# The in-projection begun at half of the tokens, and the combine of the experts' rows shared between GpSimd and VectorE

## The chip, the cores and the metric

The kernel runs on one core of one Trainium2 chip. The metric is device time in microseconds (us) from launch to end; a lower number is better. Each run is one execution of the whole program. The profile is one execution recorded by the hardware profiler; its span goes from the first to the last instruction. The engines are TensorE (PE; its weight loads are PEld), VectorE (DVE), ScalarE (ACT), GpSimd (POOL) and SyncE (SP, which here only issues DMAs).

## What is computed

One inference step of a 2-layer decoder over 576 tokens (512 of a prompt, 64 samples), model width 1024, float32. Cut to what matters here:

```python
def decoder(x, ...):
    for l in range(2):
        mix = token_mixers(rmsnorm(x, norm1_g), ...)   # z = hn @ w_in, then RG-LRU | MLA | GLA, then @ w_out
        x = x + mix
        x = x + hier_moe(rmsnorm(x, norm2_g))
    return rmsnorm(x, final_norm_g), ...

def hier_moe(t):                                       # every token goes to 2 of 32 experts
    w_sel = softmax(top_v) * g_prob                    # two weights per token
    y = sum over the 2 choices k of  w_sel[:, k] * expert_k(t)
```

`hn` is the normalised input of the mixers, `z` (1792 columns here, with padding) the in-projection.

## The kernel before, in words

The program is written by hand per engine: each engine has its own instruction list, and semaphores order them. Nothing is scheduled by a planner, except that PSUM banks are dealt out by a list: `psum_plan` names every use of a bank in order, use n lies in bank n modulo 8, `begin` waits until the bank's former use was read, `done` says it is filled, `take` waits for that, `give` says it was read, and `after` waits for the reading.

Tokens lie in five tiles `t` of 128 rows (the last has 64) in `x`. A layer begins with `norm_sums` on ScalarE (L717 squares a tile and sums it, L718 takes the root) and `norm_rows` on VectorE (L974 the reciprocal, L975 the scaled row into `xs`). TensorE transposes each tile in two groups of four (L1498, keys `("hn", t, g)`), and the groups are copied from PSUM to `hT`: group 0 by ScalarE (L706, `half_out`), group 1 by VectorE (L998), the latter after all five tiles were normalised. Only then does the in-projection start.

The in-projection runs over 14 column tiles `m` in the order of `Z_ORDER`, and for each over two halves `h` of 288 tokens, eight matmuls a block (L1528, keys `("z", m, h)`; the trace has two records for each matmul). Weights come by DMA into four buffers in turn (`win`, L445); SP loads the fifth column tile when the first one's second half has been computed. ScalarE and VectorE read the blocks out of PSUM in the same order. VectorE has a chain of small coefficient instructions ahead of that (L1004 to L1019), which waits once for ScalarE (L768).

After the mixers and the router comes the loop over blocks of experts. It leaves every token's two expert rows in `y_rows` in HBM. When all are stored, SP loads them into `ygat` with ten DMAs (L534; n = 2t + k for tile t and choice k). VectorE then combines: for each tile two instructions `x = ygat * weight + x` (L1474), one per choice, the second waiting for the first, and a memset that tells the tile is done (`combined`). One tile late it normalises (`norm_rows`) for the next layer, or, after the second layer, for the output, which SP stores tile by tile (L540). GpSimd's last instruction of a layer is `hold` (L647).

On GpSimd other work of the same kind stands in the mixers: products of masks (L610), differences (L593, L627, L632), and a cast at the start (L551).

Of the kernel before, what the change touches and what calls it, by code (L numbers as in the profile page):

```python
# [61 lines left out]
def rows_of(t):  # L62
    return P if t < TT - 1 else NS
# [114 lines left out]
def hybrid_step(nc, a, o):  # L178
# [5 lines left out]
    with ExitStack() as ctx:  # L184
# [35 lines left out]
        def cut(region, at, *dims):  # L220
# [89 lines left out]
            qpe_ready gelu gexp oacc_ready oacc_steps gsq out_b sel_exp sel_exp_done held home_copied""".split()  # L310
# [238 lines left out]
        def _(pool):  # L549
# [3 lines left out]
            for L in range(DEPTH):  # L553
# [142 lines left out]
                hold()  # L696


        @block.scalar
        def _(act):  # L700
# [3 lines left out]
            def half_out(L, kind, t):  # L704
                bk, r = take(act, L, (kind, t, 0)), rows_of(t)
                give(copy(hT[:, 0:4, t * P:t * P + r],  # L706
                          bk[:, :].rearrange("p (k n) -> p k n", k=4)[:, :, 0:r]), (kind, t, 0))

            def norm_sums(n):

                junk = cut(rb, 0, D) if n % 2 == 1 else cut(rg, 0, D)
                for t in range(TT):
                    r = rows_of(t)
                    if n == 0:
                        act.wait_ge(x_in[t], 16)
                    x_done(act, n, t)
                    link(fn(junk[:r, :], x[:r, t, :], ACT.Square, accum_out=sm[:r, t:t + 1]))  # L717
                    fn(sm[:r, 5 + t:6 + t], sm[:r, t:t + 1], ACT.Sqrt, scale=1.0 / D, bias=eps_col[:r]) \  # L718
                        .then_inc(S["ssq_ready"], 1)
                    if n % 2 == 0 and n < 2 * DEPTH and t >= 2:  # L720
                        half_out(n // 2, "hn", t - 2)
# [40 lines left out]
            for L in range(DEPTH):  # L762
                norm_sums(2 * L)
                for t in range(TT - 2, TT):
                    half_out(L, "hn", t)
# [4 lines left out]
                for m in Z_ORDER:  # L770
                    for h, cols in enumerate(halves):
                        if m in (Z_CQ, Z_CQ + 1, Z_CKV):
                            bk = take(act, L, ("z", m, h))
                            fn(sq[:, m - Z_CQ, cols], bk[:, 0:HALF], ACT.Square).then_inc(S["sq_ready"], 1)
                        elif m < Z_Y:
                            bk, key = take(act, L, ("z", m, h)), ("z", m, h)
                            if h == 0:
                                give(copy(xext[:, m, 3:3 + HALF], bk[:, 0:HALF]), key)
                            else:
                                copy(xext[:, m, 3 + HALF:XE], bk[:, 0:SEQ - HALF])  # L780
                                give(copy(xext[:, m, XE:].rearrange("p (b c) -> p b c", c=SEXT)[:, :, 3:],
                                          bk[:, SEQ - HALF:HALF].rearrange("p (b q) -> p b q", q=NQ)), key)
                        elif m < Z_CQ:
                            bk = take(act, L, ("z", m, h))
                            give(copy(yl[:, m - Z_Y, cols], bk[:, 0:HALF]), ("z", m, h))
                        elif m in (Z_GV, Z_GV + 1):
                            bk = take(act, L, ("z", m, h))
                            give(copy(gv[:, m - Z_GV, cols], bk[:, 0:HALF]), ("z", m, h))
# [174 lines left out]
        def _(dve):  # L963
# [29 lines left out]
            for L in range(DEPTH):  # L993
                if L == 0:
                    norm_rows(0, range(TT))
                for t in range(TT):
                    bk, r = take(dve, L, ("hn", t, 1)), rows_of(t)
                    give(V.tensor_copy(hT[:, 4:8, t * P:t * P + r],  # L998
                                       bk[:, :].rearrange("p (k n) -> p k n", k=4)[:, :, 0:r]), ("hn", t, 1))
# [96 lines left out]
                for m in Z_ORDER:  # L1096
                    for h, cols in enumerate(halves):
                        key = ("z", m, h)
                        if m in (Z_CQ, Z_CQ + 1, Z_CKV):
                            bk = take(dve, L, key)  # L1100
                            nsq += 1
                            dve.wait_ge(S["sq_ready"], 6 * L + nsq)
                            give(V.tensor_copy(cq[:, m - Z_CQ, cols] if m < Z_CKV else ckvT[:, cols],
                                               bk[:, 0:HALF]), key)
                        elif m == Z_PE:
                            bk = take(dve, L, key)
                            if h > 0:
                                dve.wait_ge(S["kpe_ready"], 2 * L + h)
                            V.tensor_copy(gaT[64:80, cols], bk[64:80, 0:HALF])
                            link(V.tensor_copy(ropetmp[0:32, :], bk[32:64, 0:HALF]))  # L1110
                            link(V.tensor_tensor(ropetmp[0:32, :], ropetmp[0:32, :], sin[0:32, cols], ALU.mult))
                            give(V.tensor_tensor(kpeT[0:32, cols], bk[0:32, 0:HALF], cos[0:32, cols], ALU.mult),
                                 key)
                            after(dve, L, key)
                            V.tensor_tensor(kpeT[0:32, cols], kpeT[0:32, cols], ropetmp[0:32, :], ALU.add) \
                                .then_inc(S["kpe_ready"], 1)
                        elif m in (Z_GQ, Z_GK):
                            bk = take(dve, L, key)
                            give(V.tensor_copy((gq if m == Z_GQ else gk)[:, cols], bk[:, 0:HALF]), key)
                        elif m >= Z_GO:  # L1120
                            bk = take(dve, L, key)
                            dve.wait_ge(S["tailsaved"], L + 1)
                            give(V.tensor_copy(gout[:, m - Z_GO, cols], bk[:, 0:HALF]), key)
# [344 lines left out]
                for n in range(2 * TT):  # L1468
                    t, k = n // 2, n % 2
                    r = rows_of(t)  # L1470
                    dve.wait_ge(ygat_in[n], 16 * (L + 1))
                    if k == 1:
                        dve.wait_ge(S["ygat_used"], 2 * TT * L + n)
                    ins = V.scalar_tensor_tensor(x[:r, t, :], ygat[:r, n, :], sm[:r, 100 + 5 * k + t:101 + 5 * k + t],  # L1474
                                                 x[:r, t, :], ALU.mult, ALU.add)
                    ins.then_inc(S["ygat_used"], 1)
                    if k == 1:
                        dve.wait_ge(S["ygat_used"], 2 * TT * L + n + 1)
                        V.memset(sm[:, 205:206], 0.0).then_inc(S["combined"], 1)
                        if t > 0:  # L1480
                            norm_rows(2 * L + 2, (t - 1,))
# [4 lines left out]
        def _(pe):  # L1486
# [15 lines left out]
            for L in range(DEPTH):  # L1502
                transpose_rows(L, "hn", 2 * L, range(TT))
                for t in range(TT):
                    for g in range(2):
                        after(pe, L, ("hn", t, g))
# [15 lines left out]
                for n, m in enumerate(Z_ORDER):  # L1522
                    pe.wait_ge(win_in[n % 4], 16 * (L * WUSES[n % 4] + n // 4 + 1))
                    mrows = 80 if m == Z_PE else P
                    for h, cols in enumerate(halves):
                        bk = begin(pe, L, ("z", m, h))
                        for k in range(KT):
                            ins = mm(bk[:mrows, 0:HALF], win[:, n % 4, k, :mrows], hT[:, k, cols],  # L1528
                                     start=k == 0, stop=k == KT - 1)
                        done(ins, ("z", m, h))  # L1530
# [431 lines left out]
```

## Time and profile before

| what | us |
|---|---|
| median of 3 runs | 1673.18 |
| lowest and highest run | 1669.05, 1679.38 |
| profiled execution, its own time | 1666.96 |
| its span | 1665.0 |
| TensorE busy in the span | 1343.6 (81%) |
| VectorE busy | 584.1 (35%) |
| ScalarE busy | 368.3 (22%) |
| GpSimd busy | 306.1 (18%) |

Busy shares are averages over stages that have different limits; what a change in a stage is worth is read from the waits in that stage. The in-projection of layer 0 begins at 25.46 us and that of layer 1 at 834.17 us of the span. The last instructions of the span are the normalisation after layer 1 and the stores of the output.

### The profile page before, as it was taken

Reading aid. Unit: us, or ns where it says so; the run is one execution under the profiler, and the core shown is the slowest. Engines: PE = TensorE matmul, PEld = TensorE weight load, DVE = VectorE, ACT = ScalarE, POOL = GpSimd, SP = SyncE. Lnnn points to the kernel's source line nnn. Section 1 sums busy time; section 2 is a strip of 40 time slices with the busy share of each in tenths; the row PEclk is TensorE's granted clock in tenths of the full one; section 3 lists DMA queues with packets and bytes.
Section 4 is the critical chain, followed back from the end, with each engine's and each line's share of the span. In section 5 each row is a group of like instructions: output and inputs, shape, how many; then the busy total and the mean of one; then the engine's idle time right before and its main releaser. Section 6 shows DMA issues by size and latency. Waiting matters only on the chain.

```text
span 1665.0 us, 21687 instructions
## 1 busy us (share of the span) xinstructions
PE 1343.6 (81%) x7043; PEld 782.2 (47%) x7044; DVE 584.1 (35%) x1561; ACT 368.3 (22%) x849; POOL 306.1 (18%) x713
## 2 busy tenths in 40 slices
PE   5989999868975778888499899887799578788881
PEld 4767555434453344444277664544334434344440
DVE  3272587321134111111525537851022511111115
ACT  3242124423110011111214312352302011111112
POOL 0001410000001333333100034100000033343341
PEclk9999989879966999999699899998699589999996
DMA  6210120432074899996521012024123779989745
GB/s 227 64 34 26 59 76 1 152 127 89 20 309 162 332 392 369 407 407 236 199 79 60 23 53 84 1 76 145 71 76 112 301 272 406 389 308 356 298 194 176
DMA packets 98612, 298.51 MB, mean 179 GB/s; under 512 B 13198, under 2 KB 29934, under 8 KB 98162
## 3 DMA queue, kind: packets, MB, share of 16 engines
q1 hardware_dynamic: 85138, 272.62, 43.8%
q0 software_dynamic: 13408, 25.04, 4.1%
q8 instruction: 38, 0.62, 0.2%
q14 instruction: 28, 0.23, 0.0%
HBM read 289.37 MB, written 27.09 MB: 190 GB/s over the span
## 4 chain that ended last, share of the span: by engine, by line
PE 55%; DMA 20%; DVE 12%; issue 5%; ACT 3%; POOL 2%; SPq 1%; POOLq 1%; DVEq 0%; ACTq 0%
DMA ra<-h_rows,slot_now 18%; PE bank L1528 13%; PE bank L1788 9%; PE bank L1846 5%; PE bank L1857 3%; PE bank L1828 2%; PE bank L1733 2%; PE bank L1722 2%; PE bank L1721 2%; PE bank L1550 2%; PE bank L1801 2%; PE bank L1615 1%; PE bank L1665 1%; PE bank L1669 1%; DVE x L1474 1%
## 5 line engine op out<-in xcount | busy, mean ns | idle before, releaser
L1528 PE MATMUL bank<-ra,rb 128*128 128x288 f32 (+1 forms) x896 | 224.9, 414 | 3.6 <-DVE ra L998 3.6
L1528 PEld LDWEIGHTS bank<-ra,rb 128*128 128x128 f32 (+1 forms) x896 | 171.2, 192 | 54.6 <-issue 4.2
L1467 DVE COPY rb<-bank 128x512 f32<-128x512 f32 x71 | 49.1, 692 | 222.4 <-DMA y_rows<-rb,home_now 171.7
L957 ACT ACTIVATE rb<-bank 128x128 f32<-128x128 f32 x71 | 19.7, 277 | 415.6 <-PE bank L1846 415.6
L1828 PE MATMUL bank<-cst,ra 128*128 128x128 f32 x292 | 48.8, 291 | 72.9 <-DMA ra<-h_rows,slot_now 72.9
L1846 PE MATMUL bank<-rg,rb 128*64 128x256 f32 x768 | 92.2, 395 | 7.5 <-issue 4.5
L1461 DVE TENSOR_TENSOR rb<-rb,bank 128x128 f32<-128x128 f32 x71 | 20.5, 288 | 195.5 <-ACT rb L957 195.5
L1846 PE MATMUL bank<-re,rb 128*64 128x256 f32 x736 | 85.8, 386 | 2.6 <-issue 1.2
L1857 PE MATMUL bank<-re,rb 128*64 128x512 f32 x296 | 74.5, 625 | 14.2 <-DVE rb L1463 14.2
L667 POOL DMA_INDIRECT ra<-h_rows,slot_now x73 | 77.0, 1055 | 39.7 <-issue 39.7
L1846 PEld LDWEIGHTS bank<-rg,rb 128*64 128x64 f32 x768 | 56.8, 142 | 52.8 <-issue 28.5
L656 POOL DMA_INDIRECT y_rows<-rb,home_now x71 | 73.0, 1028 | 38.9 <-issue 38.9
L1828 PEld LDWEIGHTS bank<-cst,ra 128*128 128x128 f32 x292 | 31.2, 143 | 104.0 <-DMA ra<-h_rows,slot_now 97.1
L1846 PEld LDWEIGHTS bank<-re,rb 128*64 128x64 f32 x736 | 53.7, 140 | 45.7 <-issue 24.0
L949 ACT COPY rb<-bank 128x512 f32<-128x512 f32 x73 | 42.7, 585 | 137.9 <-PE bank L1828 137.9
L641 POOL DMA_DIRECT2D h_rows<-re x4 | 2.2, 550 | 363.3 <-DVE re L975 363.3
L1721 PE MATMUL bank<-re 128*128 128x128 f32 (+3 forms) x128 | 50.1, 474 | 10.4 <-DVE rf L1249 8.4
L1857 PE MATMUL bank<-rg,rb 128*64 128x512 f32 x192 | 50.5, 650 | 9.2 <-DVE rb L1463 9.2
L1294 DVE TENSOR_REDUCE sm<-bank 128x1 f32<-128x128 f32 (+1 forms) x64 | 31.4, 490 | 64.1 <-PE bank L1723 63.0
L1722 PE MATMUL bank<-re 32*128 32x128 f32 (+3 forms) x128 | 52.9, 494 | 0.0
L1351 DVE TENSOR_TENSOR x<-x,bank 128x512 f32<-128x512 f32 (+1 forms) x20 | 13.7, 686 | 111.6 <-PE bank L1788 111.6
L1846 PE MATMUL bank<-rf,rb 128*64 128x256 f32 x448 | 51.2, 381 | 1.5 <-issue 0.7
(356 smaller groups left out, 2164.0 us busy)
## 6 DMA issues: line engine op xcount, KB each, us to landing
rg<-in_w_moe SPq DMA_DIRECT2D x24, 2048.0 KB, 11.6
re<-in_w_moe SPq DMA_DIRECT2D x20, 2048.0 KB, 13.5
re<-in_w_moe SPq DMA_DIRECT2D x30, 1024.0 KB, 15.9
rg<-in_cache SPq DMA_DIRECT2D x128, 192.0 KB, 3.6
rg<-in_w_moe SPq DMA_DIRECT2D x24, 1024.0 KB, 14.3
rf<-in_w_moe SPq DMA_DIRECT2D x10, 2048.0 KB, 13.0
ra<-in_w_moe SPq DMA_DIRECT2D x10, 2048.0 KB, 12.7
rb<-in_win SPq DMA_DIRECT2D x28, 512.0 KB, 3.7
```

Of the source, the lines that this page charges most:

```text
L656: nc.gpsimd.indirect_dma_start(y_halves, bass.IndirectOffsetOnAxis(ap=home_now[:, 0:1], axis=0), ysb, None, bounds_check=4 * T - 1, oob_is ...
L667: nc.gpsimd.indirect_dma_start(xg, None, h_halves, bass.IndirectOffsetOnAxis(ap=slot_now[:, 0:1], axis=0), bounds_check=2 * T - 1, oob_is_ ...
L949: copy(xT, bank[0][:, :].rearrange("p (k h n) -> p k h n", k=4, h=2)).then_inc(S["xt_ready"], 1)
L1467: V.tensor_copy(ysb, bank[5][:, :]).then_inc(S["y_ready"], 1)
L1528: ins = mm(bk[:mrows, 0:HALF], win[:, n % 4, k, :mrows], hT[:, k, cols], start=k == 0, stop=k == KT - 1)
L1550: ins = mm(bk[:, 0:HALF], wq[:, k, col * P:(col + 1) * P], cq[:, k, cols], start=k == 0, stop=k == 1)
L1721: mm(bk[:, 0:n], qa[:, hd, q], ckvT[:, 0:n], start=True, stop=False)
L1722: mm(bk[:, 0:n], qpe[g, hd // 4, q], kpeT[g, 0:n], start=False, stop=False)
L1788: ins = mm(bk[:r, :], merged[k][:, t * P:t * P + r], wout[n][:, k, :], start=k == 0, stop=k == 7)
L1828: ins = tr(bank[0][:, k * P:(k + 1) * P], xg[:, k * P:(k + 1) * P], ident)
L1846: ins = mm(bank[2][SLOTS * h:SLOTS * (h + 1), 0:DE], xT[:, k % 4, k // 4, :], wgu[s][:, k, h * DE:(h + 1) * DE], start=k == 0, stop=k == K ...
L1857: ins = mm(bank[5][SLOTS * n:SLOTS * (n + 1), :], actT[:, k, :], wdn[s][:, k, 512 * n:512 * n + 512], start=k == 0, stop=k == 1)
```

## The change

Three things. The in-projection's first four column tiles are computed first for the first 288 tokens (which need tiles 0, 1 and 2 only), then for the rest; tiles 3 and 4 are transposed between the blocks. All groups of transposed rows are copied by ScalarE, one tile behind the squares. And in the combine, GpSimd scales the first choice's rows and adds them to `x`, and VectorE adds the second choice's.

```diff
+def z_steps():
+    for h in range(2):
+        for m in Z_ORDER[:4]:
+            yield m, h
+    for m in Z_ORDER[4:]:
+        for h in range(2):
+            yield m, h
 def psum_plan():
-    keys = [("hn", t, g) for t in range(TT) for g in range(2)]
-    for m in Z_ORDER:
-        keys += [("z", m, h) for h in range(2)]
+    keys = [("hn", t, g) for t in range(3) for g in range(2)]
+    for m, h in z_steps():
+        keys += [("z", m, h)]
+        if h == 0 and m in Z_ORDER[:2]:
+            keys += [("hn", 3 + Z_ORDER.index(m), g) for g in range(2)]
...
 # GpSimd, after the loop over the experts' blocks
                 hold()
+                for t in range(TT):
+                    r = rows_of(t)
+                    pool.wait_ge(ygat_in[2 * t], 16 * (L + 1))
+                    nc.gpsimd.tensor_scalar(ygat[:r, 2 * t, :], ygat[:r, 2 * t, :], sm[:r, 100 + t:101 + t],
+                                            None, ALU.mult).then_inc(S["first_scaled"], 1)
+                    pool.wait_ge(S["first_scaled"], TT * L + t + 1)
+                    nc.gpsimd.tensor_tensor(x[:r, t, :], x[:r, t, :], ygat[:r, 2 * t, :], ALU.add)                         .then_inc(S["first_added"], 1)
...
 # ScalarE, norm_sums, and behind it
-                    if n % 2 == 0 and n < 2 * DEPTH and t >= 2:
-                        half_out(n // 2, "hn", t - 2)
+                    if n % 2 == 0 and n < 2 * DEPTH and t >= 1:
+                        half_out(n // 2, "hn", t - 1)
+                        half_out(n // 2, "hn", t - 1, 1)
-                for t in range(TT - 2, TT):
-                    half_out(L, "hn", t)
+                for g in range(2):
+                    half_out(L, "hn", TT - 1, g)
...
 # VectorE, start of a layer
-                for t in range(TT):
-                    bk, r = take(dve, L, ("hn", t, 1)), rows_of(t)
-                    give(V.tensor_copy(hT[:, 4:8, t * P:t * P + r],
-                                       bk[:, :].rearrange("p (k n) -> p k n", k=4)[:, :, 0:r]), ("hn", t, 1))
...
 # VectorE, the combine
-                for n in range(2 * TT):
-                    t, k = n // 2, n % 2
+                for t in range(TT):
                     r = rows_of(t)
-                    dve.wait_ge(ygat_in[n], 16 * (L + 1))
-                    if k == 1:
-                        dve.wait_ge(S["ygat_used"], 2 * TT * L + n)
-                    ins = V.scalar_tensor_tensor(x[:r, t, :], ygat[:r, n, :], sm[:r, 100 + 5 * k + t:101 + 5 * k + t],
-                                                 x[:r, t, :], ALU.mult, ALU.add)
-                    ins.then_inc(S["ygat_used"], 1)
-                    if k == 1:
-                        dve.wait_ge(S["ygat_used"], 2 * TT * L + n + 1)
-                        V.memset(sm[:, 205:206], 0.0).then_inc(S["combined"], 1)
-                        if t > 0:
-                            norm_rows(2 * L + 2, (t - 1,))
+                    dve.wait_ge(ygat_in[2 * t + 1], 16 * (L + 1))
+                    dve.wait_ge(S["first_added"], TT * L + t + 1)
+                    V.scalar_tensor_tensor(x[:r, t, :], ygat[:r, 2 * t + 1, :], sm[:r, 105 + t:106 + t],
+                                           x[:r, t, :], ALU.mult, ALU.add).then_inc(S["combined"], 1)
+                    if t > 0:
+                        norm_rows(2 * L + 2, (t - 1,))
...
 # TensorE, start of a layer
-                transpose_rows(L, "hn", 2 * L, range(TT))
-                for t in range(TT):
+                transpose_rows(L, "hn", 2 * L, range(3))
+                for t in range(3):
                     for g in range(2):
                         after(pe, L, ("hn", t, g))
-                for n, m in enumerate(Z_ORDER):
+                for m, h in z_steps():
+                    n = Z_ORDER.index(m)
+                    if h == 1 and n == 0:
+                        for t in range(3, TT):
+                            for g in range(2):
+                                after(pe, L, ("hn", t, g))
...
+                    if h == 0 and n < 2:
+                        transpose_rows(L, "hn", 2 * L, (3 + n,))
```

The lists of ScalarE and VectorE follow the same `z_steps` when they read the blocks out. In the rows below the line numbers of the changed program are its own (some 14 to 24 higher than before).

On TensorE, the start of a layer, before (`bank<-cst,re` are transposes, `bank<-ra,rb` the in-projection):

```order
L1498 MATMUL bank<-cst,re 128x128 x32
L1498 MATMUL bank<-cst,re 128x64 x8
L1528 MATMUL bank<-ra,rb 128x288 x48
L1528 MATMUL bank<-ra,rb 80x288 x16
L1528 MATMUL bank<-ra,rb 128x288 x32
```

and with the change:

```order
L1513 MATMUL bank<-cst,re 128x128 x24
L1547 MATMUL bank<-ra,rb 128x288 x8
L1513 MATMUL bank<-cst,re 128x128 x8
L1547 MATMUL bank<-ra,rb 128x288 x8
L1513 MATMUL bank<-cst,re 128x64 x8
L1547 MATMUL bank<-ra,rb 128x288 x8
L1547 MATMUL bank<-ra,rb 80x288 x8
L1547 MATMUL bank<-ra,rb 128x288 x24
L1547 MATMUL bank<-ra,rb 80x288 x8
L1547 MATMUL bank<-ra,rb 128x288 x32
```

The transposes of tiles 3 and 4 stand behind the first and the second block of the in-projection now.

On VectorE, the combine and the normalisation after it, before (`x<-re,sm,x` is a combine, `re<-x,sm,re` a normalised row):

```order
L1474 SCALAR_TENSOR_TENSOR x<-re,sm,x 128x1024 x2
L1479 MEMSET sm 128x1
L1474 SCALAR_TENSOR_TENSOR x<-re,sm,x 128x1024 x2
L1479 MEMSET sm 128x1
L974 RECIPROCAL sm<-sm 128x1
L975 SCALAR_TENSOR_TENSOR re<-x,sm,re 128x1024
```

and with the change on VectorE:

```order
L1493 SCALAR_TENSOR_TENSOR x<-re,sm,x 128x1024 x2
L998 RECIPROCAL sm<-sm 128x1
L999 SCALAR_TENSOR_TENSOR re<-x,sm,re 128x1024
L1493 SCALAR_TENSOR_TENSOR x<-re,sm,x 128x1024
L998 RECIPROCAL sm<-sm 128x1
L999 SCALAR_TENSOR_TENSOR re<-x,sm,re 128x1024
```

with, on GpSimd, behind the last `hold` of the layer (`re` holds `ygat`):

```order
L661 TENSOR_TENSOR sm<-cst 1x1
L714 TENSOR_SCALAR re<-re,sm 128x1024
L717 TENSOR_TENSOR x<-x,re 128x1024
L714 TENSOR_SCALAR re<-re,sm 128x1024
L717 TENSOR_TENSOR x<-x,re 128x1024
```

VectorE has one combine per tile instead of two, and GpSimd two instructions per tile where it had none.

On ScalarE, the squares and copies at the start of a layer, before:

```order
L717 ACTIVATE rg,sm<-x 128x1024
L718 ACTIVATE sm<-sm 128x1
L717 ACTIVATE rg,sm<-x 128x1024
L718 ACTIVATE sm<-sm 128x1
L706 COPY ra<-bank 128x4x128
L717 ACTIVATE rg,sm<-x 128x1024
```

and with the change:

```order
L738 ACTIVATE rg,sm<-x 128x1024
L739 ACTIVATE sm<-sm 128x1
L727 COPY ra<-bank 128x4x128 x2
L738 ACTIVATE rg,sm<-x 128x1024
L739 ACTIVATE sm<-sm 128x1
L727 COPY ra<-bank 128x4x128 x2
```

Both copies of tile 0 now stand ahead of the square of tile 2; before, one copy of it stood ahead of the square of tile 3.

## Rows read from the trace of the kernel before

**Rows 1.** The page, chain that ended last: shares of the span by engine.
```profile
PE 55%; DMA 20%; DVE 12%; issue 5%; ACT 3%; POOL 2%; SPq 1%; POOLq 1%; DVEq 0%; ACTq 0%
```

**Rows 2.** Chain of waits in order of time (start us, us, what).
```profile
25.46 48.49 PE bank L1528 x192
...
831.09 2.73 DVE ra L998 x5
834.17 48.61 PE bank L1528 x192
```

**Rows 3.** Timeline, layer boundary (start, us, engine, line, operation, [idle before, releaser]).
```profile
809.31 2.69 DVE L1474 SCALAR_TENSOR_TENSOR x<-re,sm,x 128x1024 f32<-128x1024 f32 x2 [7.58 <-DMA re<-y_rows]
...
812.63 2.67 DVE L1474 SCALAR_TENSOR_TENSOR x<-re,sm,x 128x1024 f32<-128x1024 f32 x2 [0.51 <-DMA re<-y_rows]
...
815.61 1.28 DVE L975 SCALAR_TENSOR_TENSOR re<-x,sm,re 128x1024 f32<-128x1024 f32 x1
...
825.35 1.97 PE L1498 MATMUL bank<-cst,re 128*128 128x128 f32 x8 [2.25 <-DVE re L975]
...
829.81 1.28 DVE L975 SCALAR_TENSOR_TENSOR re<-x,sm,re 64x1024 f32<-64x1024 f32 x1
...
830.72 0.59 ACT L706 COPY ra<-bank 128x512 f32<-128x512 f32 x1 [0.76 <-PE bank L1498]
```

**Rows 4.** GpSimd's instructions by form (shapes xcount | busy us, mean ns | idle before).
```profile
L610 POOL TENSOR_TENSOR rg<-rg,cst 128x512 f32<-128x512 f32 x16 | 16.3, 1040 | 0.0
...
L559 POOL COPY rf<-vec 128x24 f32<-128x24 f32 x4 | 0.7, 210 | 0.0
...
L551 POOL CAST mask<-rf 128x512 bf16<-128x512 f32 x1 | 0.6, 612 | 14.7 <-DMA pages<-in_page_table 14.7
L627 POOL TENSOR_TENSOR re<-rg 128x32 f32<-128x32 f32 x2 | 0.6, 298 | 7.3 <-DVE re L1241 7.3
```

**Rows 5.** Timeline, 218 to 221 us, VectorE and GpSimd in the mixers.
```profile
218.18 0.88 POOL L627 TENSOR_TENSOR re<-rg 128x384 f32<-128x384 f32 x1 [5.61 <-DVE re L1241]
218.74 0.87 DVE L1252 TENSOR_TENSOR rg<-rg,rf 128x512 f32<-128x512 f32 x1
...
219.02 0.70 POOL L632 TENSOR_TENSOR re<-rg 128x32 f32<-128x32 f32 x1
...
220.24 0.69 DVE L1252 TENSOR_TENSOR rg<-rg,rf 128x512 f32<-128x512 f32 x1
```

**Rows 6.** Timeline, end of the program.
```profile
1660.29 1.28 DVE L975 SCALAR_TENSOR_TENSOR re<-x,sm,re 64x1024 f32<-64x1024 f32 x1
```

**Rows 7.** DMA issues, 800 to 835 us (xcount, KB each, median us to landing).
```profile
re<-y_rows SPq DMA_DIRECT2D x2, 256.0 KB, 12.7
```

**Rows 8.** Timeline, start of layer 0.
```profile
17.46 1.06 ACT L717 ACTIVATE rg<-x 128x1024 f32<-128x1024 f32 x1
17.83 0.16 DVE L974 RECIPROCAL sm<-sm 128x1 f32<-128x1 f32 x1 [3.99 <-PE bank L1498]
...
18.64 0.29 ACT L718 ACTIVATE sm<-sm 128x1 f32<-128x1 f32 x1
...
20.77 1.09 PE L1498 MATMUL bank<-cst,re 128*128 128x128 f32 x8 [0.30 <-DVE re L975]
```

**Rows 9.** Windows: busy us per engine (x instructions), then PEclk, DMA share, GB/s.
```profile
834.00:836.00 2.00, 1.83 (x4) 1.44 (x5) 1.46 (x10) 0.20 (x1) 0.00 (x0) 0.50 0.18 53
...
838.00:840.00 2.00, 2.00 (x10) 1.58 (x9) 0.00 (x0) 0.00 (x0) 0.00 (x0) 1.00 0.00 0
```

**Rows 10.** The page, DMA issues of the whole run.
```profile
rb<-in_win SPq DMA_DIRECT2D x28, 512.0 KB, 3.7
```

**Rows 11.** Timeline, ScalarE's table load and VectorE's coefficient chain in layer 1.
```profile
832.58 1.28 ACT L768 ACT_TABLE_LOAD   x1
...
834.56 0.17 DVE L1008 TENSOR_SCALAR sm<-sm 128x2 f32<-128x2 f32 x1 [0.27 <-ACT sm L768]
...
837.53 0.17 DVE L1019 TENSOR_SCALAR sm<-vec 128x4 f32<-128x4 f32 x1
```

More of the change, by code:

```diff
@@ L702, in _, with half_out @@
             copy, fn = nc.scalar.copy, nc.scalar.activation
[L704 to L707, printed above, removed]
+            def half_out(L, kind, t, g=0):
+                bk, r = take(act, L, (kind, t, g)), rows_of(t)
+                give(copy(hT[:, 4 * g:4 * g + 4, t * P:t * P + r],
+                          bk[:, :].rearrange("p (k n) -> p k n", k=4)[:, :, 0:r]), (kind, t, g))
             def norm_sums(n):
@@ L769, in _ @@
                 act.wait_ge(S["pads_ready"], L + 1)
[L770 to L788, printed above, removed]
@@ new lines, in _ @@
+                for m, h in z_steps():
+                    cols = halves[h]
+                    if m in (Z_CQ, Z_CQ + 1, Z_CKV):
+                        bk = take(act, L, ("z", m, h))
+                        fn(sq[:, m - Z_CQ, cols], bk[:, 0:HALF], ACT.Square).then_inc(S["sq_ready"], 1)
+                    elif m < Z_Y:
+                        bk, key = take(act, L, ("z", m, h)), ("z", m, h)
+                        if h == 0:
+                            give(copy(xext[:, m, 3:3 + HALF], bk[:, 0:HALF]), key)
+                        else:
+                            copy(xext[:, m, 3 + HALF:XE], bk[:, 0:SEQ - HALF])
+                            give(copy(xext[:, m, XE:].rearrange("p (b c) -> p b c", c=SEXT)[:, :, 3:],
+                                      bk[:, SEQ - HALF:HALF].rearrange("p (b q) -> p b q", q=NQ)), key)
+                    elif m < Z_CQ:
+                        bk = take(act, L, ("z", m, h))
+                        give(copy(yl[:, m - Z_Y, cols], bk[:, 0:HALF]), ("z", m, h))
+                    elif m in (Z_GV, Z_GV + 1):
+                        bk = take(act, L, ("z", m, h))
+                        give(copy(gv[:, m - Z_GV, cols], bk[:, 0:HALF]), ("z", m, h))
+                    if h == 0:
+                        continue
@@ L1095, in _ @@
                 nsq = 0
[L1096 to L1123, printed above, removed]
@@ L1519, in gate_products @@
                     done(ins, ("gate", t, 2))
-                for n, m in enumerate(Z_ORDER):
-                    pe.wait_ge(win_in[n % 4], 16 * (L * WUSES[n % 4] + n // 4 + 1))
[L1524 to L1530, printed above, removed]
+                for m, h in z_steps():
+                    n = Z_ORDER.index(m)
[3 more added lines that the diff above has]
+                                after(pe, L, ("hn", t, g))
+                    pe.wait_ge(win_in[n % 4], 16 * (L * WUSES[n % 4] + n // 4 + 1))
+                    mrows, cols = 80 if m == Z_PE else P, halves[h]
+                    bk = begin(pe, L, ("z", m, h))
+                    for k in range(KT):
+                        ins = mm(bk[:mrows, 0:HALF], win[:, n % 4, k, :mrows], hT[:, k, cols],
+                                 start=k == 0, stop=k == KT - 1)
+                    done(ins, ("z", m, h))
+                    if h == 0 and n < 2:
+                        transpose_rows(L, "hn", 2 * L, (3 + n,))
+                    if h == 0:
+                        continue
                     if m == Z_X + 1:
```

33 lines of the change are left out of this document (32 added, 1 removed).

## The prediction, on record before the changed kernel ran

> **What bounds the kernel now.** I read the chain of waits by engine first: TensorE holds 55% of it, DMA 20%, VectorE 12% [rows 1]. The chain in order of time then shows where the change sits. In each layer, once the in-projection has begun, TensorE carries 192 records in a row, 48.5 to 48.6 us, with no wait between them; the 2.73 us before it belong to VectorE's five copies of transposed rows [rows 2]. So the in-projection is bound by TensorE, and moving its first matmul earlier is worth what it moves, less whatever is put between the matmuls. Ahead of it in the second layer stands the combine: the timeline shows VectorE working without a gap, per tile of 128 tokens two combining instructions (2.67 us) and one scaling of the normalised row (1.28 us), while GpSimd does nothing [rows 3]. The same combine, without an in-projection behind it, ends the program. Three places change: the start of layer 0, the boundary of the layers, the end.
>
> I call the five normalising instructions N0 to N4 (VectorE L975) and the tiles' combines C0 to C4. Before, N0 ends at 816.89, N2 at 825.3 (TensorE is released at 825.35), N4 at 831.09: from N0 to N2 8.4 us, 4.2 us a tile [rows 3].
>
> **The parts, and what each costs.**
>
> *GpSimd's two instructions.* Neither exists in the trace at 128x1024. The add has two inputs: GpSimd's TENSOR_TENSOR takes 0.298 us for 32 columns and 1.040 us for 512 [rows 4], 1.55 ns a column, so 1.83 us for 1024; its bounds are the 1.04 us of half its columns and twice that, 2.08 us. The scaling has one input: COPY takes 0.21 us for 24 columns and CAST 0.61 us for 512 [rows 4], so 1.03 us for 1024. Its bounds are the 0.61 us of half its columns and the two-input rate, 1.83 us. I take the lines, since 512 columns lie nearest. A tile then costs GpSimd 2.9 us, with a semaphore between the two. The walk below gives +6.4 us with these, -4 us with both lower bounds and +15 us with both upper ones.
>
> By rate the Trainium skill is dearer (GPSIMD Engine Reference, section 3.1, Elementwise — side-by-side cycle accounting): it gives 4497 ns for a two-input add of 2048 columns, which would be some 2.25 us for 1024, an estimate. The rows here give 1.83 us, and I keep them; with 2.25 us the whole sum below would be +9.9 instead of +6.4.
>
> *Do the two engines work at once?* The trace has one clean case [rows 5]. GpSimd's L627 runs from 218.18 to 219.06. VectorE's L1252, two inputs in SBUF, begins at 218.74 and takes 0.87 us; the same instruction with GpSimd idle takes 0.69 us at 220.24. It lost the time up to GpSimd's end. Then GpSimd's 32-column L632, begun at 219.02, takes 0.70 us where 32 columns take 0.30 us [rows 4]: it ended just after VectorE's (219.61). Each engine stood until the other's instruction was over. So I count the two as excluding each other while they move data. All of VectorE's work in the combine (C and N) has two inputs in SBUF, so it is all subject to this.
>
> The rows show this for TENSOR_TENSOR alone, and VectorE's instruction here is SCALAR_TENSOR_TENSOR. The Trainium skill (SBUF — State Buffer, section Who interferes with whom) says that a VectorE instruction with two SBUF inputs contends with any GpSimd instruction that reads SBUF, and for its whole length; by it my sum stands at +6.4, and if that were not so the rival of overlap would hold, at -4.9.
>
> *The boundary, walked.* The first choice's rows of tile 0 land as now, 809.3; tile 1's at 812.6 [rows 3]. GpSimd scales 809.35 to 810.4 and adds until 812.3; C0 then runs 812.4 to 813.7, where before both combines were over at 812.0. GpSimd's scaling of tile 1 is held by C0 until 814.5, its add ends at 816.4, and its next scaling goes at once, until 817.4. C1 waits for that and ends at 818.6. Then add (820.1), N0 (821.3), scaling (822.1), C2 (823.3), add (824.8), N1 (826.0) and so on, in turn. A tile now costs GpSimd's data time 0.88 + 1.58 plus twice VectorE's 1.12, 4.7 us in all against 4.2 us before. (I take 0.15 and 0.25 us of GpSimd's two and some 0.16 us of VectorE's as start and end that exclude nobody: the intercepts of the lines above, and VectorE's 0.17 us for an instruction of two columns [rows 11].) N2 ends at 830.7, N3 at 833.5, N4 at 835.1: VectorE finishes **4.0 us later** than 831.09. The rows of tile 4 land 12.7 us after an issue near 809.9 [rows 7], 822.6, before GpSimd wants them (824.8).
>
> *The earlier in-projection.* It needs tiles 0 to 2 alone. After N2 come eight transposes, 1.97 us [rows 3], the second copy on ScalarE, 0.59 us [rows 3], and 0.35 us from the last copy to the first matmul (833.82 to 834.17 [rows 2]): 3.0 us with the semaphores, so the first matmul goes at 833.7, 0.5 us earlier than now. Against that the transposes of tiles 3 and 4, which hide behind VectorE today, now stand between matmuls: 1.09 us each at the high clock [rows 8], 2.2 us for both. They are ready by then (N3 at 833.5, N4 at 835.1; the first block of matmuls lasts until 839.6). The clock is no difference: at the start of the in-projection the granted clock is 0.50, the 1.2 GHz level, and 1.00 from 838 on [rows 9]; the first block will again come at the low level, behind the same kind of transposes at the same level. Boundary: -0.5 + 2.2 = **+1.7 us**.
>
> *Layer 0.* There is no combine. ScalarE now copies tile 0's both halves before it squares tile 2. The second half is transposed at 17.8 (VectorE was released by it at 17.83 [rows 8]), so ScalarE is through at 18.4; Square to Sqrt takes 1.47 us (17.46 to 18.93 [rows 8]), so N2 runs until 21.5 instead of 19.3. Its transposes end at 22.6, ScalarE's copies at 23.65, and the first matmul goes at 24.0 against 25.46: -1.45. With the 2.2 us of transposes: **+0.7 us**.
>
> *The end.* No in-projection follows; the last row is normalised 4.0 us later (1660.29 plus 1.28 before [rows 6]) and its store behind it: **+4.0 us**.
>
> *At nothing.* VectorE's ten copies move to ScalarE, which waits for TensorE there; the memset and a wait per tile go. SP's load of vec and the four weight loads behind it wait for the first combine: 1.6 us later, and more than 15 us ahead of the first matmul. The six loads behind the fifth combine are issued from 832 on instead of 828, for uses behind the 192 records. GpSimd's pads for layer 1 stand behind its own adds, 4 us later, and are wanted at the first evacuation. Weight buffer 0 is free after five blocks of matmuls instead of two, and its next load is wanted after eight: 11.6 us of blocks, and a load lands in 3.7 us [rows 10]. Bank 6 is closer: its second use is the fifth block, 19.7 us after the first matmul (12 blocks in 48.6 us with a slow first one: 3.9 us each and about 5.9 for the first, and the 2.2 us of transposes). ScalarE has tile 4 copied 12.4 us in, loads a table (1.28 us), and VectorE's chain of small coefficient instructions (834.56 to 837.70, 3.1 us) stands ahead of its copies [rows 11]: the bank is free at 17.6 us. Cover 2.1 us.
>
> **Sum:** +0.7 + 1.7 + 4.0 = **+6.4 us**. The profiled execution took 1666.96 us (span 1665.0), which becomes 1673.4; it lies 6.2 us under the median of the runs, 1673.18, which becomes **1680**. A measurement of this kernel can tell about 1% (17 us) from no change, so this is "no change".
>
> **The rivals.**
>
> *The engines overlap.* If a SCALAR_TENSOR_TENSOR is not held, GpSimd paces the tiles at 2.9 us and the landings do the rest: C0 still at 813.7, N2 at 824.5, N4 at 830.0. The first matmul goes at 827.5: -6.7 + 2.2 at the boundary, -1.1 at the end, +0.7 in layer 0: -4.9 us, **1668**. For it: no row shows this instruction held. Against it: the held one also has two SBUF inputs. 14%.
>
> *GpSimd is the bound, slower.* If the scaling by a column of scalars runs at the two-input rate (1.83 us) and the add takes 2.08 us, with exclusion, a tile costs 5.8 us; N2 ends at 834.1, N4 at 840.4: +5.1 at the boundary, +9.3 at the end, +0.7: +15 us, **1688**. The point from which GpSimd hurts at all is 2.0 us of its data time per tile (4.2 less VectorE's 2.24); it decides for "slower" from about 4.1 us of its time per tile, where I count 2.9. For it: no row has a one-input arithmetic instruction. Against it: CAST at 0.61 us. 12%.
>
> *Bank 6 is late.* If the coefficient chain came 4 us later than counted, the fifth block would wait 2 us in each layer: +10.4, **1684**. The cover is thin but every piece has a row. 5%.
>
> **How the numbers follow.** My forecast 66%, the rivals 14, 12 and 5%, something unseen 3%. The range runs from the overlap (1668) to the slow GpSimd (1688) and a little past both, since single runs of one kernel scatter from 1669 to 1679: 1666 to 1691. Forecast, overlap and bank 6 all lie within 1%; the slow rival stands just at its edge, so a good half of it counts as slower, with the unseen on either side: faster 3%, within 1% 89%, slower 8%.
>
> **What would show it.** GpSimd's adds near 1.8 us and scalings near 1.0 us when alone, and either stretched to 2 us or more behind VectorE; C1 to C3 and N0 to N2 near 2.0 to 2.5 us instead of 1.28 us; the first matmul of layer 1 near its old time, with two groups of eight transposes between blocks; the last normalisation 4 us later counted from the landing of the first rows. I am wrong if C and N keep 1.28 us beside a busy GpSimd, if GpSimd's pair is far from 2.9 us, or if the fifth block of matmuls waits.

## The result and the profile after

| | before | changed |
|---|---|---|
| median, us (lowest to highest, 7 runs each) | 1675.51 (1669.05 to 1680.15) | 1687.14 (1683.74 to 1691.76) |
| the profiled execution, us (its span) | 1666.96 (1665.0) | 1684.45 (1682.6) |

The ratio is **1.0081**, 95% interval 1.0056 to 1.0106: slower by 13.6 us of 1675.5 (9.4 to 17.8). That is within 1%, as forecast (the interval's upper end lies just above 1%), and twice the 6.4 us that were summed. One run of e_early2 (6568 us) and one of the kernel before among those of the first four experiments (7096 us) are slow runs and stand in none of the ratios below.

The page's shares of the chain that ended last, after (before: [rows 1]):

```profile
PE 54%; DMA 19%; DVE 10%; issue 6%; POOL 5%; ACT 3%; SPq 1%; POOLq 1%; DVEq 0%; ACTq 0%
```

GpSimd (POOL) rose from 2 to 5%, VectorE (DVE) fell from 12 to 10%. The chain in order of time at the layer boundary says where (start us, us, what; L714 is GpSimd's scaling, L717 its add, L1493 VectorE's combine C, L999 the normalising N, L1547 the in-projection):

```profile
807.18 3.56 DMA re<-y_rows
...
810.84 2.86 POOL re L714
...
813.77 2.34 POOL x L717
816.11 2.83 POOL re L714
...
819.01 2.34 POOL x L717
821.35 2.83 POOL re L714
...
824.25 2.87 POOL x L717
827.12 2.83 POOL re L714
...
830.03 2.88 POOL x L717
...
838.51 0.59 ACT ra L727
839.11 0.44 issue
839.54 5.72 PE bank L1547 x16
845.26 0.87 PE bank L1513 x8
846.13 3.88 PE bank L1547 x16
850.02 0.64 PE bank L1513 x8
850.66 39.00 PE bank L1547 x160
...
894.67 15.58 PE bank L1547 x64
```

Nothing but GpSimd's own two instructions stands between the landing of the first rows (810.74) and the end of tile 3's add (832.91), for which C3 and, behind it, N2 wait: a tile costs 5.24 us (816.11 to 821.35), then 5.77 us (821.35 to 827.12), where VectorE alone needed 4.2 [rows 3]. The timeline of the same stretch shows how the two engines stand to each other:

```profile
810.84 2.85 POOL L714 TENSOR_SCALAR re<-re,sm 128x1024 f32<-128x1024 f32 x1 [5.08 <-DMA re<-y_rows]
813.77 2.34 POOL L717 TENSOR_TENSOR x<-x,re 128x1024 f32<-128x1024 f32 x1
...
821.33 2.84 POOL L714 TENSOR_SCALAR re<-re,sm 128x1024 f32<-128x1024 f32 x1
821.46 2.05 DVE L1493 SCALAR_TENSOR_TENSOR x<-re,sm,x 128x1024 f32<-128x1024 f32 x1 [3.19 <-POOL x L717]
823.62 1.28 DVE L999 SCALAR_TENSOR_TENSOR re<-x,sm,re 128x1024 f32<-128x1024 f32 x1
824.25 2.87 POOL L717 TENSOR_TENSOR x<-x,re 128x1024 f32<-128x1024 f32 x1
```

Read it in three steps. The first two rows are GpSimd's instructions with VectorE idle: 2.85 and 2.34 us, where the prediction took 1.03 and 1.83. The combine, begun 0.13 us after a scaling, takes 2.05 us instead of 1.28: it stands 0.77 us. But N0 keeps its 1.28 us although the same scaling still runs until 824.17: in these rows a scaling of 2.84 us keeps VectorE away only in its first part. The add that begins under N0 is stretched from 2.34 to 2.87 us, by 0.53 us of the 0.65 us that N0 still has.

Set out by stretches of the two profiled executions (us; the group of 64 is the last row of the chain above, 64 records of the same line that follow the long run of the in-projection and some small groups: it begins at 78.97 and 887.80 before, 79.07 and 894.67 after; a combining instruction is, after, GpSimd's scaling too):

| stretch | before | after | difference | in the prediction |
|---|---|---|---|---|
| start to the group of 64, layer 0 | 78.97 | 79.07 | +0.1 | +0.7 |
| from there to the first combining instruction | 730.34 | 731.77 | +1.4 | none |
| from there to the group of 64, layer 1 | 78.49 | 83.83 | +5.3 | +1.7 |
| from there to the first combining instruction of the end | 752.04 | 752.32 | +0.3 | none |
| from there to the end of the last N | 21.73 | 32.25 | +10.5 | +4.0 |

The three places that the change touches sum to 15.9 us, inside the interval. The two long stretches between them hold no instruction of the combine; over all profiled kernels of this document they scatter by 7 and 8 us, with no clear order in it. The first stretch scatters too, from 77.4 to 80.5 us among the kernels whose in-projection is as before (the kernel before, e_pool, e_probe), so its +0.1 us is no gain and no loss that one profile can tell. The end's two rows, after (before: [rows 6]), the first of the combine and the last N:

```profile
1646.99 2.85 POOL L714 TENSOR_SCALAR re<-re,sm 128x1024 f32<-128x1024 f32 x1 [4.78 <-DMA re<-y_rows]
...
1677.97 1.27 DVE L999 SCALAR_TENSOR_TENSOR re<-x,sm,re 64x1024 f32<-64x1024 f32 x1
```

### The profile page after: what moved, and what is told of

Read it like the earlier page. It is cut to its first block, busy times and chain, and to the rows that moved or that the text cites. A ratio compares the mean times of both kernels' runs of the same rounds, so it can differ in the third digit from the quotient of the medians.

```text
span 1682.6 us, 21716 instructions
## 1 busy us (share of the span) xinstructions
PE 1338.4 (80%) x7043; PEld 780.0 (46%) x7044; DVE 570.6 (34%) x1531; ACT 373.0 (22%) x859; POOL 362.2 (22%) x733
## 4 chain that ended last, share of the span: by engine, by line
PE 54%; DMA 19%; DVE 10%; issue 6%; POOL 5%; ACT 3%; SPq 1%; POOLq 1%; DVEq 0%; ACTq 0%
DMA ra<-h_rows,slot_now 17%; PE bank L1547 13%; PE bank L1811 8%; PE bank L1869 5%; PE bank L1880 3%; PE bank L1851 2%; PE bank L1756 2%; PE bank L1745 2%; PE bank L1573 2%; PE bank L1744 2%; PE bank L1824 2%; POOL re L714 2%; PE bank L1638 1%; PE bank L1688 1%; PE bank L1692 1%
## 5 line engine op out<-in xcount | busy, mean ns | idle before, releaser
L1547 PE MATMUL bank<-ra,rb 128*128 128x288 f32 (+1 forms) x896 | 226.7, 416 | 1.9 <-ACT ra L727 1.9
L1547 PEld LDWEIGHTS bank<-ra,rb 128*128 128x128 f32 (+1 forms) x896 | 171.3, 192 | 53.7 <-issue 3.0
L1869 PEld LDWEIGHTS bank<-rg,rb 128*64 128x64 f32 x768 | 56.8, 142 | 52.9 <-issue 28.7
L1513 PE MATMUL bank<-cst,re 128*128 128x128 f32 (+1 forms) x112 | 18.9, 333 | 47.7 <-DVE re L999 32.0
L1880 PE MATMUL bank<-rg,rb 128*64 128x512 f32 x192 | 46.5, 605 | 9.2 <-DVE rb L1484 9.2
## 6 DMA issues: line engine op xcount, KB each, us to landing
rg<-in_w_moe SPq DMA_DIRECT2D x24, 1024.0 KB, 13.6
```

The lines of the kernel that those rows point to most:

```text
L1869: ins = mm(bank[2][SLOTS * h:SLOTS * (h + 1), 0:DE], xT[:, k % 4, k // 4, :], wgu[s][:, k, h * DE:(h + 1) * DE], start=k == 0, stop=k == K ...
L1880: ins = mm(bank[5][SLOTS * n:SLOTS * (n + 1), :], actT[:, k, :], wdn[s][:, k, 512 * n:512 * n + 512], start=k == 0, stop=k == 1)
```

## The experiments

Three theories. **A**: the loss is the length of GpSimd's own two instructions, one after the other, and the early in-projection by itself is a small gain. **B**: the loss is that the two engines exclude each other. **C**: the reordered in-projection costs.

**The early in-projection alone** (e_early): the changed kernel with the combine as it was, all ten combining instructions on VectorE.

```diff
-                    dve.wait_ge(S["first_added"], TT * L + t + 1)
...
+                    ins = V.scalar_tensor_tensor(x[:r, t, :], ygat[:r, n, :], sm[:r, 100 + 5 * k + t:101 + 5 * k + t],
+                                                 x[:r, t, :], ALU.mult, ALU.add)
```

> The in-projection's half of the change alone; the combine is VectorE's, as before. Theory A (GpSimd's own two instructions, 2.84 and 2.34 us alone, cost the time; the early in-projection is a small gain): against before, layer 0 +0.1 us, boundary -5.9 us for the earlier first matmul and +1.75 us for the transposes between the blocks, end 0: -4 us, ratio 0.9975. Theory C (the in-projection's reordering costs, the shared combine less than it seems): +2 us or more, ratio 1.001 or above.

Measured: ratio 0.9978 (0.9956 to 1.0000), median 1666.48 beside 1673.12. First rows to first matmul 19.4 us (811.00 to 830.36) instead of 24.9; 2.4 us of the 5.5 are given back before the group of 64 (56.0 us behind the first matmul instead of 53.6): 1.5 us are the transposes of tiles 3 and 4, and the rest stands in the first block, 6.61 us long, which begins at the granted clock of 0.50 (rows below). C asked for a ratio of 1.001 or more and falls: the reorder by itself gains, 3.7 us by the ratio, whose interval just reaches no gain.

**GpSimd's share alone** (e_pool): the in-projection as it was, the combine as in the changed kernel.

> The combine's half of the change alone; the in-projection starts after all five tiles, as before. Theory A: from the landing of the first rows to the last normalised row 32.3 us instead of 21.8, and nothing of it is hidden: +10.5 us at the boundary and +10.5 us at the end, +21 us, ratio 1.0125. Theory C: at most what the whole change cost, less what the in-projection costs: +12 us or less, ratio 1.007 or below.

Measured: 1.0137 (1.0098 to 1.0175), median 1692.85. GpSimd's scaling is 2845 ns in the mean here too, its add 2600, and the first matmul goes 35.4 us behind the first rows, 10.5 us later than before, as A said. Its chain (L700 is the scaling, L1529 the in-projection):

```profile
808.70 2.86 POOL re L700
...
844.11 48.39 PE bank L1529 x192
```

The loss belongs to GpSimd's share, and the early in-projection hides part of it (10.5 us at the boundary here, 5.3 in the whole change), since it does not wait for tiles 3 and 4.

**ScalarE scales, GpSimd only adds** (e_act): the rest as changed.

```diff
-                    nc.gpsimd.tensor_scalar(ygat[:r, 2 * t, :], ygat[:r, 2 * t, :], sm[:r, 100 + t:101 + t],
-                                            None, ALU.mult).then_inc(S["first_scaled"], 1)
...
 # ScalarE, norm_sums: tiles 0 and 1 ahead of the first square, tiles 2 to 4 each ahead of a later one
+                        for u in ((0, 1), (2,), (3,), (4,), ())[t]:
+                            act.wait_ge(ygat_in[2 * u], 16 * (n // 2))
+                            fn(ygat[:rows_of(u), 2 * u, :], ygat[:rows_of(u), 2 * u, :], ACT.Copy,
+                               scale=sm[:rows_of(u), 100 + u:101 + u]).then_inc(S["first_scaled"], 1)
```

> The whole change, but ScalarE scales the first choice's rows (about 1.06 us a tile), and GpSimd only adds. Theory A: GpSimd's pace falls from 5.8 to between 2.4 and 4.4 us a tile, VectorE's combines and normalisations still exclude its adds; N2 ends 16 to 21.5 us after the first rows land instead of 25.6, N4 21.5 to 26 us instead of 32.3: between -4.5 and +5.5 us against before, 8 to 18 us faster than the whole change. Theory B (the standstill of the two engines against each other is what costs, not GpSimd's rate): the adds still collide with twice as many VectorE instructions, so the time stays within 3 us of the whole change, ratio 1.006 to 1.010.

Measured: 1.0031 (1.0007 to 1.0056), median 1675.8, 5.2 us over the kernel before: the upper edge of A's range (-4.5 to +5.5 us), and under B's (1.006 and more), which the interval leaves out. The timeline of a tile (L737 ScalarE's scaling, L714 the add, L1495 C, L1001 N):

```profile
824.02 1.28 DVE L1495 SCALAR_TENSOR_TENSOR x<-re,sm,x 128x1024 f32<-128x1024 f32 x1 [2.31 <-POOL x L714]
824.25 1.15 ACT L737 ACTIVATE re<-re,sm 128x1024 f32<-128x1024 f32 x1
825.42 1.28 DVE L1001 SCALAR_TENSOR_TENSOR re<-x,sm,re 128x1024 f32<-128x1024 f32 x1
825.48 3.44 POOL L714 TENSOR_TENSOR x<-x,re 128x1024 f32<-128x1024 f32 x1 [1.56 <-ACT re L737]
```

The scaling takes 1.15 us there, but waits behind squares and copies on ScalarE; GpSimd idles 1.56 us for it, and the add then stands behind N (3.44 us instead of 2.34). A tile takes 5.0 us (C at 824.02 and 829.02): better than 5.77, but more than the 2.4 to 4.4 us that A gave for the pace, and still worse than VectorE's 4.2.

**A shorter scaling on GpSimd** (e_bcast): the same product as a two-input TENSOR_TENSOR with the weight broadcast.

```diff
-                    nc.gpsimd.tensor_scalar(ygat[:r, 2 * t, :], ygat[:r, 2 * t, :], sm[:r, 100 + t:101 + t],
-                                            None, ALU.mult).then_inc(S["first_scaled"], 1)
+                    nc.gpsimd.tensor_tensor(ygat[:r, 2 * t, :], ygat[:r, 2 * t, :],
+                                            sm[:r, 100 + t:101 + t].to_broadcast([r, D]), ALU.mult) \
+                        .then_inc(S["first_scaled"], 1)
```

> The whole change, but GpSimd scales with TENSOR_TENSOR, the weight broadcast along the row, instead of TENSOR_SCALAR. Theory A: if GpSimd's time per tile sets the pace and TENSOR_SCALAR is the slow one, the scaling takes 2.3 us instead of 2.84, each tile 0.5 us less: about 1.5 us at the boundary and 2.5 us at the end, 4 us faster than the whole change, ratio to before 1.0057. Theory B: no difference to the whole change, since the collisions stay the same.

Measured: 1.0127 (1.0085 to 1.0169), median 1690.91. Both theories missed (1.0057, and no difference to 1.0081). The timeline (L714 scaling, L718 add, L1494 C, L1000 N):

```profile
812.72 1.89 POOL L714 TENSOR_TENSOR re<-re,sm 128x1024 f32<-128x1024 f32 x1 [5.18 <-DMA re<-y_rows]
814.69 2.34 POOL L718 TENSOR_TENSOR x<-x,re 128x1024 f32<-128x1024 f32 x1
...
824.10 3.21 POOL L718 TENSOR_TENSOR x<-x,re 128x1024 f32<-128x1024 f32 x1
...
825.21 3.19 DVE L1000 SCALAR_TENSOR_TENSOR re<-x,sm,re 128x1024 f32<-128x1024 f32 x1
827.28 2.87 POOL L714 TENSOR_TENSOR re<-re,sm 128x1024 f32<-128x1024 f32 x1
...
828.32 2.91 DVE L1494 SCALAR_TENSOR_TENSOR x<-re,sm,x 128x1024 f32<-128x1024 f32 x1
830.23 3.21 POOL L718 TENSOR_TENSOR x<-x,re 128x1024 f32<-128x1024 f32 x1
```

Alone the scaling is 0.96 us shorter (1.89). From the first N to the last add every instruction of both engines is stretched, and a tile takes 6.13 us (824.10 to 830.23). The prediction's sum of data times, with the measured lengths and its own start and end parts, is 1.74 + 2.09 + 2 x 1.12 = 6.07 us: here the exclusion sets the pace. So A alone is not the whole: by the traces (5.77 against 6.13 us a tile) the slow TENSOR_SCALAR was the milder of the two, since it frees VectorE early. The ratios of the two kernels overlap in their intervals and do not settle the order.

**The last layer combined by VectorE** (e_end): otherwise the changed kernel (waits left out).

```diff
-                for t in range(TT):
+                for t in range(TT if L < DEPTH - 1 else 0):
...
+                        V.scalar_tensor_tensor(x[:r, t, :], ygat[:r, 2 * t, :], sm[:r, 100 + t:101 + t],
+                                               x[:r, t, :], ALU.mult, ALU.add).then_inc(S["ygat_used"], 1)
```

> The whole change at the boundary between the layers, while the last layer's combine is VectorE's own, as before the change. Theory A (GpSimd's two instructions are in the chain of waits at both places, +10.5 us of them at the end): the stretch from the last layer's first landing to the end of the last norm is back at 21.7 to 22.2 us, and the program is about 3 us (the +13.6 measured less 10.5) over the one before, ratio 1.000 to 1.0045. Rival D (the cost lies elsewhere, spread over the layers, in the reordered in-projection or in the expert loop, where the profile of the changed kernel also had some us more): the ratio stays at 1.006 or above.

Measured: 1.0039 (1.0018 to 1.0061), median 1677.77 beside 1669.97, in A's range; the end is short again, 21.0 us (first combining instruction at 1654.51, last N over at 1675.50), a little under the 21.7 that A gave. Its interval and that of the changed kernel (1.0056 to 1.0106) just meet, so the end's 10.5 us stand on the traces, and the runs agree with them within their scatter.

**The instructions by themselves** (e_probe): the kernel before, and behind its last output GpSimd's instructions alone, then the scaling, the add and the copy each started together with four VectorE instructions back to back (semaphores left out here, and `w` is `sm[:, 100:101]`). Its time is longer by the probe and isn't compared.

```diff
+    G.tensor_scalar(ygat[:, 0, :], ygat[:, 0, :], w, None, ALU.mult)
+    G.tensor_scalar(ygat[:, 1, 0:512], ygat[:, 1, 0:512], w, None, ALU.mult)
+    G.tensor_copy(ygat[:, 2, :], ygat[:, 0, :])
+    G.tensor_tensor(ygat[:, 3, :], ygat[:, 3, :], ygat[:, 1, :], ALU.add)
...
+    V.scalar_tensor_tensor(ygat[:, 4 + k, :], ygat[:, 4 + k, :], w, x[:, k, :], ALU.mult, ALU.add)   # k = 0..3
```

> The kernel before, with a probe behind the last output (so the time of the program is longer by the probe and says nothing): GpSimd instructions alone, then each started together with four VectorE instructions back to back. Theory A (GpSimd's one-input scaling is slow by itself and keeps VectorE away only in its first 0.8 us or so, the two-input add for nearly its whole length): scaling of 128x1024 alone 2.84 us, of 512 columns about half of it; with VectorE's two-input instructions beside it the scaling stays 2.84 and one of VectorE's is stretched by about 0.8 us, the others stay 1.28; beside the add, VectorE's are stretched by some 2 us in sum or the add by as much. Rival B (an instruction of GpSimd keeps VectorE away for its whole length): beside the scaling VectorE's instructions are stretched by some 2.5 us in sum. With VectorE's one-input instructions both theories leave it open which of them stretch; if none does, the exclusion is between instructions that read two operands from SBUF.

Its timeline, alone first, then beside VectorE's two-input instructions (L1520), last one of VectorE's one-input instructions beside a scaling (L1523):

```profile
1669.75 2.85 POOL L705 TENSOR_SCALAR re<-re,sm 128x1024 f32<-128x1024 f32 x1 [30.03 <-DVE sm L1524]
...
1672.69 1.56 POOL L707 TENSOR_SCALAR re<-re,sm 128x512 f32<-128x512 f32 x1
1674.32 1.04 POOL L709 COPY re<-re 128x1024 f32<-128x1024 f32 x1
...
1675.44 2.34 POOL L711 TENSOR_TENSOR re<-re 128x1024 f32<-128x1024 f32 x1
...
1677.86 1.26 POOL L713 TENSOR_TENSOR re<-re 128x512 f32<-128x512 f32 x1
1679.15 1.28 DVE L1520 SCALAR_TENSOR_TENSOR re<-re,sm,x 128x1024 f32<-128x1024 f32 x1 [1.25 <-POOL re L713]
1679.22 3.93 POOL L716 TENSOR_SCALAR re<-re,sm 128x1024 f32<-128x1024 f32 x1
...
1680.36 2.14 DVE L1520 SCALAR_TENSOR_TENSOR re<-re,sm,x 128x1024 f32<-128x1024 f32 x1
...
1682.42 1.27 DVE L1520 SCALAR_TENSOR_TENSOR re<-re,sm,x 128x1024 f32<-128x1024 f32 x1
...
1684.99 3.46 DVE L1520 SCALAR_TENSOR_TENSOR re<-re,sm,x 128x1024 f32<-128x1024 f32 x1
1685.03 2.34 POOL L718 TENSOR_TENSOR re<-re 128x1024 f32<-128x1024 f32 x1 [1.89 <-DVE re L1520]
...
1698.66 1.61 DVE L1523 TENSOR_SCALAR re<-re,sm 128x1024 f32<-128x1024 f32 x1
```

A scaling is 2.85 us and a copy of the same rows 1.04. Begun after VectorE, the scaling stood 1.08 us until VectorE's first instruction was over (a miss of theory A, which had it at 2.84 in any company); then VectorE's second was held 0.86 us and its next, at 1682.42, not at all, while the scaling ran until 1683.15. The add held VectorE's for 2.18 us, nearly its length. Theory B for the scaling (2.5 us held) falls. Beside VectorE's one-input instructions the scaling held two of four, the second and the last (1.61 and 1.51 us instead of 0.75), so that "only in its first part" is shown for two-input instructions alone.

**Tile 2's N ahead of tile 3's combine** (e_early2): e_early, and VectorE normalises tile 2 before it combines tile 3, as ScalarE copies it before the square of tile 3.

```diff
 # ScalarE
+                            outs = ((), (0,), (1, 2), (), (3,))[t]
...
 # VectorE; the last layer keeps its order
-                        norm_rows(2 * L + 2, (t - 1,))
...
+                            ready = ((), (0,), (1, 2), (), (3,))[t]
+                        norm_rows(2 * L + 2, ready)
```

> The early in-projection alone, with VectorE's combine as before, and N2 put ahead of tile 3's first combine at the boundary (VectorE: C0 C1 N0 C2 N1 N2 C3 N3 C4 N4 in pairs of combines), tile 2's copies on ScalarE ahead of the square of tile 3. By the trace of the early in-projection alone, N2 begins at 825.98 behind C3 and could begin at about 823.2, when tile 2's square root is done. Theory A (the path to the first matmul is VectorE's order): first matmul about 16.7 us after the first landing against 19.4, ratio to the kernel before 0.995 to 0.9975, 1 to 3 us under the early in-projection alone. Rival C (what the first half-block gains is given back by a lower clock of its matmuls or by waiting for tiles 3 and 4): ratio stays at 0.998 or above.

Measured: **0.9944** (0.9924 to 0.9964), median 1660.26 beside 1669.97: faster than the kernel before and the changed one, and just past A's range (0.995 to 0.9975); rival C falls. A had the first matmul right, 16.25 us behind the first rows for 16.7. What it had not counted is the first block, which takes 4.12 us where the kernel with the early in-projection alone had 6.61. Timelines, e_early2 first (L1519 transposes, L1553 in-projection), then e_early:

```profile
825.88 3.39 PE L1519 MATMUL bank<-cst,re 128*128 128x128 f32 x16 [2.21 <-DVE re L996]
...
830.24 4.12 PE L1553 MATMUL bank<-ra,rb 128*128 128x288 f32 x16 [0.98 <-ACT ra L720]
```

```profile
830.36 6.61 PE L1546 MATMUL bank<-ra,rb 128*128 128x288 f32 x16 [1.07 <-ACT ra L720]
```

The windows give the clock (us, busy time of PE, PEld, DVE, ACT, POOL with counts, then PEclk, DMA share, GB/s): e_early2 first, then e_early, both from 830 to 832.

```profile
830.00:832.00 2.00, 1.76 (x7) 1.44 (x8) 1.83 (x4) 1.45 (x3) 0.00 (x0) 1.00 0.76 303
```

```profile
830.00:832.00 2.00, 1.64 (x4) 1.24 (x5) 1.82 (x4) 1.44 (x3) 0.60 (x7) 0.50 0.50 106
```

With the transposes of tiles 1 and 2 in one piece ahead of it, the in-projection began at the 2.4 GHz level; e_early's, behind eight transposes after a gap, began at 1.2 GHz. That is what stood ahead, and no rule: the kernel before has 16 transposes in one piece too, then 1.58 us without work, and its in-projection began at 1.2 GHz [rows 9]:

```profile
829.57 3.01 PE L1498 MATMUL bank<-cst,re 128*128 128x128 f32 x16 [2.25 <-DVE re L975]
```

From the first rows to the group of 64 e_early2 takes 70.1 us (813.99 to 884.13) against 78.5: 8.4 us, with which the ratio (9.4 us) agrees.

## Why the prediction was right in its number and wrong in its sum

- **The class and the range held**: 1687.14 lies in 1666 to 1691, and the change is under 1%. The forecast itself was 1680; of the 7.1 us above it 2.3 are the kernel before, whose median rose from 1673.18 to 1675.51 with more runs. Of the +6.4 us the terms came out as +0.1, +5.3 and +10.5 instead of +0.7, +1.7 and +4.0. The range held because it had been drawn past the slow rival (1688). By the prediction's own sign, "if GpSimd's pair is far from 2.9 us", its mechanism was wrong: the pair takes 5.2 us.
- **The step that failed** is "The scaling has one input: COPY takes 0.21 us for 24 columns and CAST 0.61 us for 512 [rows 4], so 1.03 us for 1024". The 1.03 is right for a copy, 1.04 in the probe. A TENSOR_SCALAR is no copy: 2.85 us, above even the upper bound, 1.83, which was the two-input rate. That bound rested on an untested step, that an instruction with one tensor input is no slower than one with two. Why this one takes 2.85 us stays open.
- **The add** was mis-sized less, 2.34 for 1.83, above its bound of 2.08 too. The line through 32 and 512 columns of other instructions fell short; the probe has 1.26 us at 512 columns for this form, where [rows 4] have 1.04. The Trainium skill (GPSIMD Engine Reference, section 3.1, Elementwise — side-by-side cycle accounting) was nearer with its rate, 2.25 us for these columns by estimate.
- **The pace** was to be the sum of both engines' data times, 4.7 us a tile. That mechanism is real (e_bcast), but in the changed kernel another one decides: GpSimd's two instructions one after the other, 2.84 and 2.87 us. The sum with measured sizes would be 0.77 + 2.09 + 2 x 1.12 = 5.1 us, under the 5.77 seen. So the rival "GpSimd is the bound, slower", at 12%, had the right pace (5.8) and nearly the right loss (+15), with other parts: a scaling of 1.83, and full exclusion. That its loss comes so near is in part luck.
- **The exclusion** was right for the add and for C (2.05 us, foretold 2.0 to 2.5), wrong for N, which keeps 1.28 us. The row that it was read from [rows 5] showed less than was taken from it: VectorE's L1252 lost 0.18 us (0.87 for 0.69) of the 0.32 us for which GpSimd's L627 still ran, not all of it. The Trainium skill (SBUF — State Buffer, section SBUF: two separate sides) has the shared pair of ports held for the whole instruction; by the runs that is so for the two-input add (2.18 of 2.34 us in the probe) and not for TENSOR_SCALAR (0.77 to 0.86 of 2.85 beside two-input instructions). The rival of overlap is refuted by the same rows.
- **The early in-projection**: its first matmul was to come 0.5 us earlier and came 3.8 us later (28.7 us behind the first rows, against 24.9), all of it through the pace; the transposes between the blocks cost 1.5 us in the chain, counted as 2.2. In layer 0 the first matmul came 1.3 us earlier (24.12 for 25.46), foretold 1.45, and the transposes took the 1.5 us back: the +0.1 us, which lies within the scatter.
- **What stayed at nothing did**: the fifth block did not wait for bank 6 (160 records in 39.00 us without a break in either layer).

## What to carry to other kernels

Before handing an instruction to an idle engine, find its own duration there for this operation and this shape; a copy's rate is not a scaling's, and without a row the upper bound belongs well above the nearest known form. VectorE multiplies and adds in one instruction of 1.28 us; the split needs two on GpSimd, 5.2 us, of which at least 2.9 keep VectorE out, so each tile costs more of the shared time than it frees. What did pay was order: start the consumer at what is ready, and put the producer of its last piece ahead of work that nobody waits for.

## What the runs showed of the hardware beyond what was expected

- GpSimd's scaling by a column of scalars at 128x1024 takes 2.85 us, its product with the same column broadcast as second input 1.89, its copy 1.04.
- An instruction of 2.85 us held VectorE for 0.77 to 0.86 us, one of 2.34 us for 2.18: length says little about how long an engine excludes the other.
- VectorE's one-input TENSOR_SCALAR, 0.75 us alone in the probe, is not exempt: four beside GpSimd's scaling took 1.155 us each in the mean, two of them 1.61 and 1.51.
- The granted clock at the first matmul was not the same in every order. In e_early2 it rose within the 16 transposes (0.79 over 828 to 830 us) and was 1.00 after 0.98 us of idle; after eight transposes (e_early) it was 0.50, and in the kernel before, after 16 and 1.58 us of idle, 0.50 too. The first block took 4.12 us at 1.00 and, begun at 0.50, 5.72 us in the changed kernel and 6.61 in e_early. What decides the level is not shown.
